# Weight splits at the head of each attention place, the softmax division at its end, and a rotation behind the pairs

## The reference

```python
logits = einsum('bqhd,bkhd->bhqk', q, k) * scale + bias_or_mask
p = softmax(logits)
o = einsum('bhqk,bkhd->bqhd', p, v)
```

## Time and profile before

| | |
|---|---|
| runs (3), median | 948.94 us (947.95 to 950.07) |
| profiled execution | 947.03 us |
| its span, first to last instruction | 945.3 us |
| granted TensorE clock, mean | 0.996 |
| PE busy | 921.3 us, 97% |
| DVE busy | 580.8 us, 61% |
| ACT busy | 481.7 us, 51% |
| layer 0, places 0 to 18 | about 45 to 127 us |
| layer 1, places 11 to 32 | about 359 to 434 us |

### The profile page before, as it was taken

How to read it: one execution, slowest core, us unless ns; L and a number is a source line. 1 busy time by engine, 2 the same in 40 slices (tenths; PEclk the granted TensorE clock), 3 DMA queues, 4 the chain that set the end, 5 groups by cost and what they waited for, 6 DMA issues and landing times.

```text
span 945.3 us, 12122 instructions
## 1 busy us (share of the span) xinstructions
PE 921.3 (97%) x4502; PEld 760.8 (80%) x4502; DVE 580.8 (61%) x960; ACT 481.7 (51%) x781; POOL 32.1 (3%) x48
## 2 busy tenths in 40 slices
PE   6989999999999999999999999999999999999997
PEld 5868878888888888877888888877888888888875
DVE  4776777655553865668855556385646666564665
ACT  4856555544443555666544445355455654644434
POOL 1100025000000001000000000000000000000000
PEclk9999999999999999999999999999999999999999
DMA  8653375855554546345665555453553455355551
GB/s 305 248 179 112 112 234 151 291 180 180 188 197 163 183 142 226 128 139 196 215 202 187 186 191 199 152 200 134 181 201 132 150 199 161 113 199 179 183 177 64
DMA packets 46760, 169.20 MB, mean 179 GB/s; under 512 B 5384, under 2 KB 5536, under 8 KB 46064
## 3 DMA queue, kind: packets, MB, share of 16 engines
q1 hardware_dynamic: 44064, 156.09, 49.4%
q0 software_dynamic: 2640, 12.35, 4.2%
HBM read 167.36 MB, written 1.06 MB: 178 GB/s over the span
## 4 chain that ended last, share of the span: by engine, by line
PE 89%; ACT 4%; DVE 4%; DMA 1%; issue 1%; DVEq 0%; SPq 0%; ACTq 0%
PE psum L614 18%; PE psum L566 18%; PE psum L571 17%; PE psum L568 17%; PE psum L691 3%; PE psum L685 3%; PE psum L681 3%; PE psum L538 2%; DVE base_lo L1297 1%; PE psum L836 1%; ACT base_hi L1001 1%; PE psum L867 1%; PE psum L733 1%; PE psum L850 1%; ACT pair_probs L1094 1%
## 5 line engine op out<-in xcount | busy, mean ns | idle before, releaser
L1297 DVE TENSOR_TENSOR base_lo<-stage,base_hi 128x1024 fp32r<-128x1024 f32 (+3 forms) x223 | 261.6, 1198 | 122.5 <-ACT base_hi L1001 121.3
L1001 ACT CAST base_hi<-stage 128x1024 fp32r<-128x1024 f32 (+3 forms) x223 | 223.2, 1032 | 60.7 <-PE psum L571 32.9
L566 PE MATMUL psum<-base_hi,xt_hi 128*128 128x512 f32 (+3 forms) x528 | 209.0, 396 | 1.9 <-ACT base_hi L1001 1.6
L568 PE MATMUL psum<-base_lo,xt_hi 128*128 128x512 f32 (+3 forms) x528 | 202.1, 383 | 0.4 <-DVE base_lo L1297 0.4
L571 PE MATMUL psum<-base_hi,xt_lo 128*128 128x512 f32 (+3 forms) x528 | 202.5, 384 | 0.0
L566 PEld LDWEIGHTS psum<-base_hi,xt_hi 128*128 128x128 f32 x528 | 99.8, 189 | 22.0 <-issue 3.1
L571 PEld LDWEIGHTS psum<-base_hi,xt_lo 128*128 128x128 f32 x528 | 99.6, 189 | 18.3 <-DVE xt_lo L1337 0.4
L568 PEld LDWEIGHTS psum<-base_lo,xt_hi 128*128 128x128 f32 x528 | 99.9, 189 | 17.8 <-DVE base_lo L1297 1.1
L1297 DVE TENSOR_TENSOR extra_lo<-stage,extra_hi 128x1024 fp32r<-128x1024 f32 (+1 forms) x68 | 80.7, 1214 | 46.5 <-ACT extra_hi L1001 46.3
L1001 ACT CAST extra_hi<-stage 128x1024 fp32r<-128x1024 f32 (+1 forms) x68 | 69.0, 1045 | 42.7 <-PE psum L614 26.6
L566 PE MATMUL psum<-extra_hi,xt_hi 128*128 128x512 f32 x160 | 63.2, 395 | 0.0
(11 more groups left out here) (197 smaller groups left out, 1322.9 us busy)
## 6 DMA issues: line engine op xcount, KB each, us to landing
stage<-in_w_up SPq DMA_DIRECT2D x80, 512.0 KB, 4.4
stage<-in_w_down SPq DMA_DIRECT2D x44, 512.0 KB, 4.3
stage<-in_w_cd_in SPq DMA_DIRECT2D x28, 440.0 KB, 4.0
stage<-in_w_in_a SPq DMA_DIRECT2D x24, 512.0 KB, 4.8
stage<-in_w_in_b SPq DMA_DIRECT2D x16, 512.0 KB, 3.7
stage<-in_w_ab_in SPq DMA_DIRECT2D x12, 480.0 KB, 6.3
ln_par<-in_ln POOLq DMA_DIRECT2D x4, 1024.0 KB, 7.5
stage<-in_w_ab_out SPq DMA_DIRECT2D x8, 512.0 KB, 3.6
```

Source lines behind the costliest of these rows:

```text
L566: pe.matmul(acc, ah, wh, start=(k == 0), stop=False)
L568: pe.matmul(acc, ah, wl, start=False, stop=False)
L1001: act.copy(w_hi(c, 0, w), stage_of(c, w)).then_inc(hi_done, 1)
L1297: dve.tensor_tensor(w_lo(c, 0, w), stage_of(c, w), w_hi(c, 0, w).bitcast(F32), ALU.subtract).then_inc(lo_done, 1)
```

## The change

At each place ACT and DVE now make the split of the place's chunk first, ahead of the pair work. The bound `first_over_heads` keeps them from splitting the chunks of the feed-forward part this early, as their slots lie over the heads' data. On DVE the division moves from the head of the place ahead of stage 2 to the end of the place behind stage 1, behind mask and copy (`one_past`). With the usual rhythm, that is from the start of place n+3 to the end of place n+2. The rotation of MLA's queries goes behind the pair work of place 5. PE's order and SP's and POOL's code are not changed, and no instruction is added or removed.

```diff
-def next_stage(place, stage):
+def one_past(place, stage):
     order = L0_PLACES if place in L0_PLACES else L1_PLACES
-    at = order.index(place) + 1
-    return at_stage(order[at], stage) if at < len(order) else []
+    at = order.index(place)
+    return at_stage(order[at - 1], stage) if at else []
+
+def first_over_heads(name):
+    return GEMMS["up1" if name[:2] == "cd" else "up0"].c0
...
             def attend(name, n):
+                split_to(min(done["due"], first_over_heads(name)))
                 for p in at_stage((name, n), 3):
                     split_out(p)
                 for p in at_stage((name, n), 2):
                     copy_probs(p)
-                split_to(done["due"])
                 for p in at_stage((name, n), 1):
                     exp_pair(p)
...
             def attend(name, n):
-                for p in next_stage((name, n), 2):
-                    scale_pair(p)
+                split_to(min(done["due"], first_over_heads(name)))
                 for p in at_stage((name, n), 3):
                     rest_out(p)
                 for p in at_stage((name, n), 1):
                     mask_pair(p)
                 for p in at_stage((name, n), 0):
                     copy_pair(p)
+                for p in one_past((name, n), 1):
+                    scale_pair(p)
...
                 dve.nop().then_inc(mla_ready, 1)
-                attend("ukv", 0)
-            gemm("ukv", None, {0: mla_queries, **attending("ukv", 1)})
+            gemm("ukv", None, {0: lambda: [attend("ukv", 0), mla_queries()], **attending("ukv", 1)})
```

More of the change, by code:

```diff
@@ L1285, in _ @@
         def _(dve):
-            done = {"chunks": 0, "steps": 0}
+            done = {"chunks": 0, "steps": 0, "due": 0}
             def settle(ins):
@@ L1309, in gemm @@
                     for n in range(j * cps, (j + 1) * cps):
+                        done["due"] = ahead(g.c0 + n)
                         if evacuate is not None and n == (j + 1) * cps - 1:
@@ L1317, in gemm @@
                             between[n]()
-                        split_to(ahead(g.c0 + n))
+                        split_to(done["due"])
             def turn(name, hi, lo, k0=0, tiles=range(TT)):
@@ L1350, in wide @@
                 for k in range(g.kc):
+                    done["due"] = min(ahead(g.c0 + k), g.c0 + g.kc + beyond)
                     if between and k in between:
                         between[k]()
-                    split_to(min(ahead(g.c0 + k), g.c0 + g.kc + beyond))
+                    split_to(done["due"])
             def halves(name, t, evacuate, which=range(2)):
```

## The result

The changed kernel runs in 962.86 us (median of 4, 962.53 to 963.96), the kernel before in 949.34 beside it. The ratio is 1.0149, with a 95% interval of 1.0136 to 1.0162: 13.5 us slower. The forecast was 961.4 us.

The account below looks back on a forecast made before the run. PE, busy 97%, bounds the kernel, so only its idle time is at stake. Layer 0 4.9 us longer plus layer 1 7.6 gives 12.5 on 947.0, 959.5; adding 1.9 to reach the median, 961.4, range 953.5 to 968.

Parts of the forecast that it names:

- the main mechanism: Both attention layers: copies behind DVE's split, behind ACT's high part and exponential, make PE wait; 12.5 us slower, chance 0.82.
- The first wait: Layer 0, pair 1: PE wants the copy at 54.62 but it ends at 58.8, so 4.2 us are lost.
- The ring: Layer 1, DVE and ACT steps from copy to copy: 8.3 us, 9.2 with emptying, against PE's 7.74 per pair.
- Every pair loses 0.6 us: Layer 1: each pair late by 0.6 us, up to 1.4 with an emptying, unless something else slows PE.
- a sign of being wrong: Layer 1: a pair distance of 7.7 us as before would mean the sum of steps between copies was wrong.
- The gains: Shorter mask waits and half clock in layer 0, fewer low-part stops at both layers' ends: together 7.5 us.
- The 3.0 us wait: Layer 0, ahead of a pair's transposes, at 67.63: falls to 0.7 us, and 1.7 us of lower clock go.
- The late divisions: End of layer 1: the division, now behind a split, costs PE 0.9 us at pair 14, 1.2 at pair 15.
- "I take nothing" for the clock: Layer 0, clock after the new 4.2 us wait: no cost counted; bounds nothing and 1.7 us.
- The copy of pair 9: Layer 1: a new PE wait of 0.6 us for this copy.
- the lower clock: Rival: three or four new waits of 1 to 1.5 us each followed by 1.7 us lower clock; 967 us, chance 0.1.
- The faster case: Rival: copies are on time, so only the 7.5 us of gains show; 941.4 us, chance 0.05.

Follow-up runs that it names:

- the cut there: The changed kernel with ACT making the next place's high part ahead of the exponential, DVE's order as changed: 944.50 us, 0.9957 of the kernel before.
- the one with the transposes in the wait: The changed kernel with 36 identity transposes into an unused bank on PE ahead of pair 1's multiplication: 960.74 us, 1.0127 of the kernel before.

## Why the prediction was right, point by point

**The direction and the main mechanism** were right. The copy behind the split behind ACT's high part is what PE waits for in nine places, 12.6 of the 16.6 us of new waits for copies, probabilities and divisions. That the split on DVE is the one harmful part is shown by its removal (942.2 us), and that it harms through the exponential ahead of ACT's high part by the cut there (944.5 us).

**The first wait.** Forecast: high part at 55.9, low part at 57.0, copy done at 58.8, 4.2 us. Measured 56.04, 57.12, PE at 59.00, 4.15.

**The ring.** Forecast 8.3 us from copy to copy; measured on DVE, with the table out of the way, 8.18. What it costs PE in plain pairs of layer 1 was not as stated. "Every pair loses 0.6 us" does not hold for the leg from pair 10 to pair 11 in the changed kernel:

```profile
386.77 0.93 PE L841 MATMUL psum<-qk_t 64*128 64x128 f32 x8
...
394.52 0.93 PE L841 MATMUL psum<-qk_t 64*128 64x128 f32 x8
```

That is 7.75 us, as before, which the prediction had named as a sign of being wrong. It had also named the exception, "as long as PE is not slowed by something else": PE had just lost 2.85 us and then run at half clock, and by my reading that gave the lists of DVE and ACT the time to catch up. In the run with the constant mask, where the table was not waited for, that leg took 8.2, and PE lost the difference at `turn_probs`, to the mask. For MLA the forecast was on time without an emptying and 1.4, 1.1 and 0.8 late in the three places with one; `sum_pair` waited there 1.26, 0.94 and 0.81.

**The gains.** 1.2 and 1.5 us at the ends of the layers came as stated: from `sum_pair` of the last pair to the transposes of x took 12.13 and takes 10.94 in layer 0, 10.94 and 9.48 in layer 1. The 3.0 us wait became one of 1.0 (forecast 0.7), with no half clock behind it. All gains together are 6.2 us by the run with DVE's split last, where 7.5 were forecast.

**The late divisions** of pairs 14 and 15: forecast 0.9 and 1.2, measured 0.83 and 1.07 (for the second, the prediction's own 7.5 less 6.4 gives 1.1). The wait for the probabilities of pair 10, forecast 1.5, was 0.96.

Two terms were mis-sized, both too small. They are 3.9 us of the way from 12.5 to the profile's 15.7, and smaller terms of the other sign take 0.7 back (layer 0 6.0 for 4.9, layer 1 9.9 for 7.6). *"I take nothing" for the clock* behind the new 4.2 us wait: PE's next 1.6 us of pair work and a chunk of 4.0 us cost 2.5 us at half clock, and the 0.9 us wait that was to absorb them vanished; net 1.6, in place of nothing, within the bound of 1.7. *The copy of pair 9, "0.6"*, was 2.85 us: the mask of pair 8 started 2.3 us later than I had it, since the decay table was late. In the kernel before DVE waited 1.4 us for the table too, and it cost PE nothing, since the mask was in no ring; I had left it out of the walk. How late the table comes differs from trace to trace (below), so part of this term is the chance of one execution. And the half clock that followed took the place of the loss that I had given to pair 10. The medians lie only 13.5 to 13.9 us apart. That the forecast of 961.4 came within 1.5 us of the median is in part luck, as terms of both signs were off by more.

Of the rivals, the lower clock had a part in two places; it was not the main loss. The faster case was wrong for this order and right for its neighbours: with the split last on DVE the gains stood alone, at 942.2 us, where that case had 941.4.

What was incomplete is the account of the ring: I wrote that before "the lateness of a mask was hidden by a whole chunk", and took the copy for the necessary link. The run with the copy first shows a second way to lose, through mask and division (a ring of 7.6 us, 8.5 with an emptying). With it alone the split on DVE still cost 13.0 of its 20.6 us, so the link to the copy was not even the larger half.

## What to carry to other kernels

When in-order engines hand work to each other, average shares of busy time (61% and 51% here) say nothing about a move within a list: add up the ring of steps from one hand-over to the next of its kind and set it against the period of the engine that bounds. A step that is not urgent, as a split three chunks ahead, belongs behind the urgent ones on the consumer of its product, or its producer has to run it before anything that waits. Try the parts of such a change alone: here three of four were gains, and the fourth hid them.

## Not expected

- From the issue of the decay table's transfer to GpSimd's first step on it took between 8.4 and 11.4 us over the traces (8.6 before the change, 11.4 after it), and the moment of the issue does not explain that: the changed kernel and the one with the transposes in the wait issued it at 359.0 alike, and it took 11.4 in one and 8.5 in the other. In the kernel with only the division moved, where the mask is in no ring, 3.8 us from the multiplication of pair 8 to its mask cost PE at most 0.9 us (waits of 0.5 and 0.4 in layer 1); in the changed kernel 3.3 us were followed by the 2.85 us wait.
- A wait of PE of 2.85 us was followed by half clock for more than 3 us; the 1.5 us wait of the kernel before was not.
- DVE's split ahead with ACT's list as before costs 47 us, with ACT's split ahead too some 20 against the version with it last: the orders of the two lists are not independent.
